# Two-layer decoder trunk: selection scores as stacked one-pass products, values two steps behind, first weight tiles in pieces

## What is computed

```python
s = jnp.einsum('bqghd,bgqkd->bghqk', qb, k_g) * scale      # selection
p = masked_softmax(s, valid)
o_sel = jnp.einsum('bghqk,bgqkd->bqghd', p.astype(v_g.dtype), v_g)
s = jnp.einsum('bqghd,bkgd->bghqk', qb, k_w) * scale       # window
s = jnp.einsum('bqghd,bngd->bghqn', qb, k_cmp) * scale     # compressed
o = gb[..., 0:1] * o_cmp + gb[..., 1:2] * o_sel + gb[..., 2:3] * o_win
```

## Time and profile before

| | |
|---|---|
| median of 3 runs | 720.13 us (717.53 to 721.34) |
| profiled execution | 720.99 us, its span 719.3 us |
| TensorE, share of the span busy | 96% |
| VectorE, ScalarE | 58%, 55% |
| granted TensorE clock, mean | 0.987 |
| sparse attention, four turns | 78.6 to 169.5 us |
| latent attention, four turns | 433.6 to 507.0 us |

### The profile page before, as it was taken

One profiled execution on the slowest core, in us unless ns is written; L12 is line 12 of the kernel. 1 busy time (PEld: TensorE's weight loads), 2 busy tenths in 40 slices (PEclk: granted clock), 3 DMA queues, 4 the chain that ended last, 5 costly groups with the idle time before them and its releaser, 6 DMA issues. The chain is left out here.

```text
span 719.3 us, 9969 instructions
## 1 busy us (share of the span) xinstructions
PE 687.6 (96%) x3553; PEld 576.6 (80%) x3553; DVE 415.7 (58%) x866; ACT 395.7 (55%) x779; POOL 13.2 (2%) x36
## 2 busy tenths in 40 slices
PE   5999899999999999999998999999999999999996
PEld 4888788778778888888887998877878888888885
DVE  4786545777665555455458675454575444445555
ACT  5785646677564344433366576685673334444443
POOL 5000000000000000000000000000000000000000
PEclk9999999999999999999999999997999999999999
DMA  8854305113355555555553353524227554445431
GB/s 299 285 155 124 92 4 176 59 60 118 102 191 176 175 178 185 201 196 195 201 161 120 100 158 125 176 67 133 96 91 243 191 175 176 175 175 175 175 117 58
DMA packets 54481, 108.92 MB, mean 151 GB/s; under 512 B 2273, under 2 KB 16657, under 8 KB 54449
## 3 DMA queue, kind: packets, MB, share of 16 engines
q1 hardware_dynamic: 53536, 105.73, 43.9%
q0 software_dynamic: 912, 2.78, 1.3%
HBM read 107.46 MB, written 1.05 MB: 151 GB/s over the span
## 5 line engine op out<-in xcount | busy, mean ns | idle before, releaser
L281 DVE TENSOR_TENSOR w_lo<-raw,w_hi 128x2048 fp32r<-128x2048 f32 (+6 forms) x111 | 207.8, 1887 | 71.7 <-ACT w_hi L273 71.5
L289 PE MATMUL bank<-w_hi,act_lo 128*128 128x512 f32 (+4 forms) x504 | 198.6, 394 | 5.4 <-DVE w_lo L1885 3.9
L291 PE MATMUL bank<-w_hi,act_hi 128*128 128x512 f32 (+4 forms) x504 | 189.4, 376 | 0.0
L290 PE MATMUL bank<-w_lo,act_hi 128*128 128x512 f32 (+4 forms) x504 | 189.3, 376 | 0.0
L273 ACT ACTIVATE w_hi<-raw 128x2048 fp32r<-128x2048 f32 (+6 forms) x111 | 174.1, 1589 | 10.0 <-PE bank L291 8.9
L289 PEld LDWEIGHTS bank<-w_hi,act_lo 128*128 128x128 f32 x504 | 95.9, 190 | 25.1 <-issue 7.7
L290 PEld LDWEIGHTS bank<-w_lo,act_hi 128*128 128x128 f32 x504 | 96.1, 191 | 17.5 <-issue 1.9
L291 PEld LDWEIGHTS bank<-w_hi,act_hi 128*128 128x128 f32 x504 | 95.7, 190 | 17.1
L1306 ACT ACTIVATE hidT_hi<-bank 128x512 fp32r<-128x512 f32 x20 | 12.0, 598 | 164.0 <-PE bank L768 164.0
L1728 DVE TENSOR_TENSOR hidT_lo<-bank,hidT_hi 128x512 fp32r<-128x512 f32 x20 | 13.8, 691 | 130.1 <-ACT hidT_hi L1306 130.1
L289 PE MATMUL bank<-w_hi,hidT_lo 128*128 128x512 f32 x160 | 63.3, 396 | 0.0
(11 more groups left out here) (214 smaller groups left out, 915.3 us busy)
## 6 DMA issues: line engine op xcount, KB each, us to landing
raw<-in_w_gate_up SPq DMA_DIRECT2D x44, 1024.0 KB, 5.2
raw<-in_w_down SPq DMA_DIRECT2D x22, 1024.0 KB, 4.9
raw<-in_nsa_w_in SPq DMA_DIRECT2D x5, 1024.0 KB, 6.3
raw<-in_w_q_up SPq DMA_DIRECT2D x8, 576.0 KB, 3.9
raw<-in_nsa_w_out SPq DMA_DIRECT2D x4, 1024.0 KB, 5.4
raw<-in_mla_w_out SPq DMA_DIRECT2D x4, 1024.0 KB, 5.2
raw<-in_mla_w_in SPq DMA_DIRECT2D x4, 768.0 KB, 4.5
raw<-in_nsa_w_in SPq DMA_DIRECT2D x6, 384.0 KB, 3.3
```

The lines of the kernel that those rows point to most:

```text
L281: ins = dve.tensor_tensor(lo[:, cols], raw[s][:, cols], hi[:, cols].bitcast(F32), ALU.subtract)
L289: pe.matmul(dst, a_lo, b_hi, start=start, stop=False)
L290: pe.matmul(dst, a_hi, b_lo, start=False, stop=False)
L291: return pe.matmul(dst, a_hi, b_hi, start=False, stop=stop)
```

## The change

Scores of the sparse layer: q is split into hi (fp32r) and lo, and both halves are stacked on 128 rows; the keys' hi is stored twice on 128 rows, their lo as well. One fp32r matmul over 128 rows gives (q_hi + q_lo) k_hi for both branches, one more per key tile adds the product with k_lo. The compressed keys are stacked alike and scored in one pass with both halves beside each other (30 columns), added by VectorE. The keys' halves are made on ScalarE and VectorE, transposed in two rounds of 16, and copied out by ScalarE in eight copies. ScalarE writes each turn's queries twice (four copies for two), VectorE makes the lo part (`q_low`). The query transposes move one step later, the last one into the next turn. Values are issued two steps behind the probabilities in both layers, with a third probability buffer. `out_factors` and `taken` move to step 6 in the sparse layer, the compressed exponential ahead of `exps`. At the start the first half of weight tile 0 is split in two pieces and tile 1 in two halves; TensorE issues 5 products of zeros ahead of the first transposes and 9 behind them, and GpSimd clears their operand first. GpSimd no longer clears `qT`, `kT` and `kcT`.

```diff
@@ start, GpSimd, TensorE, ScalarE, VectorE
+            pool.memset(zero[:].bitcast(F32), 0.0).then_inc(sem("zero"), 1)
-            for a in (qT[:], kT, kcT, cT, vbd):
+            for a in (cT, vbd):
+            pe.wait_ge(sem("zero"), 1)
+            idle_products(5)
+                if s == 0:
+                    idle_products(9)
+                            if s == 0 and t == 0:
+                                pe.wait_ge(sem("second_lo" if k else "first_lo"), 1)
+                        if s == 0 and t == 0 and k == 1:
+                            pe.wait_ge(sem("first_lo"), 2)
+            for k in range(2):
+                act.activation(w_hi[0][:, k * 512:(k + 1) * 512], raw[0][:, k * 512:(k + 1) * 512], ACT.Copy) \
+                    .then_inc(sem("first_hi"), 1)
-            split_hi(act, 1, SLOT)
+            split_hi(act, 1, SLOT, part=0).then_inc(sem("second_hi"), 1)
+            split_hi(act, 1, SLOT, part=1)
@@ def scores
+                    pe.matmul(dst, q, k_hi[:, turn, :, 0:keys], start=True, stop=False)
+                    for kt in range(t + 1):
+                        last = pe.matmul(dst[:, :, kt * P:(kt + 1) * P], q, (k_lo0, k_lo1)[kt][:, turn], start=False,
+                                         stop=kt == t)
@@ def cmp_scores
-                        last = pe.matmul(bank[5][:, at_:at_ + NCMP], queries["nsa"][turn % 2][:, i, t * P:(t + 1) * P],
-                                         kcT[:, turn * NCMP:(turn + 1) * NCMP], start=True, stop=True)
+                        last = pe.matmul(bank[5][:, at_:at_ + 2 * NCMP], queries["nsa"][turn % 2][:, i, t * P:(t + 1) * P],
+                                         kc_halves[:, turn].rearrange("p v n -> p (v n)"), start=True, stop=True)
@@ def attend, TensorE
+                    if turn * UNITS + n > 1:
+                        pe.wait_ge(sem(f"{m}_probsT"), turn * UNITS + n - 1)
-                    if unit > 0:
-                        values(m, unit - 1)
+                    if unit > 1:
+                        values(m, unit - 2)
@@ query transposes
+            def turn_nsa_queries(turn, n):
+                if n == 0 and turn > 0:
+                    turn_queries("nsa", turn, 3, turned_at(n))
+                if 1 <= n < 4 and turn < TURNS - 1:
+                    if n == 1:
+                        pe.wait_ge(sem("nsa_roped"), turn + 2)
+                    turn_queries("nsa", turn + 1, n - 1, turned_at(n))
@@ keys, TensorE and ScalarE
+            def turn_halves(half):
+                pe.wait_ge(sem("ks_halves"), half + 1)
+                for j in range(2 * T):
+                    b, t = divmod(j, T)
+                    for g in range(QUAD):
+                        last = pe.transpose(K_BANKS[4 * half + j][:, g * P:(g + 1) * P],
+                                            ks_halves[half][:, t, b * QUAD + g, :], ident[:])
+                    last.then_inc(sem("k_turned"), 1)
-            pe.wait_ge(sem("kT_out"), 1)
+            pe.wait_ge(sem("kT_out"), 4)
             turn_hidc(0)
+            turn_halves(1)
+            for t in range(T):
+                ins = copy(twice(ks_halves[0][:, t]).bitcast(F32R), to_both(kstage[:, t]))
@@ head of attention
+            block_values()
             pe.wait_ge(sem("nsa_roped"), 1)
...
-                    if turn == 0 and at_ == 0 and n == 0:
-                        block_values()
-                        pe.wait_ge(sem("nsa_q_out"), (turn + 2) * T)
+                        pe.wait_ge(sem("nsa_q_out"), (turn + 2) * 2 * T)
+            split_hi(act, NSA_Q1 + 3, 3 * KVW)
+            exps("nsa", 0)
+            exps("nsa", 1)
             q_out("nsa", 1, NSA_Q1 + 2)
@@ VectorE
+            def q_low(to):
+                hi, lo = (a.rearrange("p t i n -> p (t i) n") for a in q_halves(to))
+                dve.wait_ge(sem("nsa_q_out"), to * 2 * T + 2 * T)
+                chain.link(dve.tensor_copy(hi[:, :, 0:16].bitcast(F32R), lo[:, :, 0:16]))
+                dve.tensor_tensor(lo.bitcast(F32R), lo, hi, ALU.subtract).then_inc(sem("nsa_roped"), 1)
+            for t in range(T):
+                ins = dve.tensor_tensor(twice(ks_halves[1][:, t]).bitcast(F32R), to_both(kstage[:, t]),
+                                        twice(ks_halves[0][:, t]), ALU.subtract)
-                    if n == 7:
+                    if n == (6 if nsa else 7):
                         out_factors(m, turn, 0)
                         taken(m, turn, 0)
```

More of the change, by code:

```diff
@@ L56 @@
 SLOT = 2048
+BIG = 10208
 SEL_SCALE = HD ** -0.5
@@ L172, in trunk, with place @@
         newton = sb("newton", [P, 2])
-        with nc.sbuf_tensor("big", [P, 10240], F32) as big:
+        with nc.sbuf_tensor("big", [P, BIG], F32) as big:
             pass
+        with ExitStack() as within:
+            def place(name, shape, dt=F32):
+                return within.enter_context(nc.sbuf_tensor(name, shape, dt))
+            k_lo1 = place("k_lo1", [P, QUAD, 2, P], F32R)
+            k_hi = place("k_hi", [P, QUAD, 2, SEQ], F32R)
+            place("to_q_odd", [P, 3072])
+            q_odd = place("q_odd", [P, QUAD, SEQ], F32R)
         more_hi = [sb(f"more_hi{i}", [P, SLOT], F32R) for i in range(2)]
@@ L1002, in turn_keys, with idle_products @@
                 last.then_inc(sem("mla_k_turned"), 1)
+            def idle_products(count):
+                for _ in range(count):
+                    pe.matmul(bank[7][:], zero[:, 0:P], zero[:], start=True, stop=True)
             pe.wait_ge(sem("ident"), 1)
+            pe.wait_ge(sem("zero"), 1)
+            idle_products(5)
             def kv_block(b):
@@ L1538, in _ @@
                 .then_inc(sem("gelu_done"), 1)
+            for j in range(2 * T):
+                keys_halves_out(1, j)
             act.wait_ge(sem("hidc_turned"), 2)
@@ L1840, in attend @@
                         masked(m, turn * UNITS + n)
+                    if nsa and n == 0 and 0 < turn < TURNS - 1:
+                        q_low(turn + 1)
                     if turn > 0:
@@ L1883, in _ @@
             turn_dve(dve, 0, 0, [0])
-            dve.wait_ge(sem("first_hi"), 1)
-            dve.tensor_tensor(w_lo[0][:, 0:SLOT // 2], raw[0][:, 0:SLOT // 2], w_hi[0][:, 0:SLOT // 2].bitcast(F32),
-                              ALU.subtract).then_inc(sem("first_lo"), 1)
+            for k in range(2):
+                dve.wait_ge(sem("first_hi"), k + 1)
+                cols = slice(k * 512, (k + 1) * 512)
+                dve.tensor_tensor(w_lo[0][:, cols], raw[0][:, cols], w_hi[0][:, cols].bitcast(F32),
+                                  ALU.subtract).then_inc(sem("first_lo"), 1)
             turn_dve(dve, 0, 0, [1])
@@ L1889, in _ @@
             split_lo(dve, 0, SLOT, part=1)
-            split_lo(dve, 1, SLOT)
+            dve.wait_ge(sem("second_hi"), 1)
+            dve.tensor_tensor(w_lo[1][:, 0:SLOT // 2], raw[1][:, 0:SLOT // 2], w_hi[1][:, 0:SLOT // 2].bitcast(F32),
+                              ALU.subtract).then_inc(sem("second_lo"), 1)
+            dve.wait_ge(hi_ready, 2)
+            split_lo(dve, 1, SLOT, part=1)
             turn_dve(dve, 0, 1)
@@ L1980, in _ @@
             rotate("nsa", 0)
+            q_low(0)
             split_lo(dve, NSA_Q1 + 2, 2 * KVW)
```

235 lines of the change are left out of this document (129 added, 106 removed).

## The result

The changed kernel took 715.85 us (median of 7 runs, 710.98 to 716.94), the kernel before 720.83 us (7 runs): a ratio of 0.993, 95% interval 0.991 to 0.996. In a second series on another chip it was 714.12 us and 0.991 (0.989 to 0.993). So the change is faster by 5 to 6.5 us. 15.9 us were forecast, 704.2 us, with 712.0 as the range's upper end.

A forecast was written before the change was run, and what follows sets the result against it. TensorE, busy for 96% of the span, was taken as the bound. The terms summed to -15.9 us, from 720.99 to 705.1 us; that execution lay 0.9 us above its median, so 704.2 us, range 695.5 to 712.

The forecast's parts named there:

- Start, -1.5: Kernel's start: split weight tiles and zero products bring the first block's products earlier, 1.5 us less, 0 to 1.6.
- Keys in halves, +1.9: Ahead of sparse attention: a second round of 16 key transposes has no cover, 1.9 us more, from 1.7 to 3.4.
- head, -0.5: Head of sparse attention: transposes of step 1 start earlier, 0.5 us less, from 1.5 less to 1.5 more.
- Scores, -9.1: Sparse attention's score units: stacked fp32r matmuls instead of float32, 9.1 us less.
- compressed scores, -3.5: Sparse attention's compressed scores: one pass of eight records instead of sixteen, 0.88 us a turn, 3.5 us less in four.
- Waits, -4.7 + 3.4: Sparse turns: waits go, turn 1 keeps its clock, 4.7 us less; new waits 3.4 us, bounds 1 to 7.
- Latent attention, -1.9: Latent attention: values two steps behind remove four waits, 1.9 us less; at worst 0 us.
- A: Sparse attention: ScalarE and VectorE hold the turns, or the stacked matmul is slower, 711 us; chance 0.2.
- C: Sparse attention: without dense matmuls the clock falls, 729 us if 25 us of work run slow; chance 0.06.
- signs for A: Sparse attention in the profile after: turn 2 over 19.5 us, with waits for exponentials.
- B: Latent attention: its lost clock comes back, up to 6.9 us to be had, 697 us; chance 0.2.

The follow-up runs named there:

- e4: Changed kernel with VectorE's masks issued one unit earlier in both attention layers: 703.16 us, 0.977 of the kernel before.
- e12: Changed kernel with masks one unit earlier and the second output piece's lower half made at step 3 instead of 4: 701.60 us, repeated 700.10 us.
- e3: Changed kernel with each sparse score product made twice: 714.79 us, 0.994 of the kernel before.
- e5: Changed kernel with zero products in TensorE's waits in the head and first two turns of sparse attention: 711.41 us, 0.988 of the kernel before.
- e9: Kernel before the change with VectorE's masks issued one unit earlier in both attention layers: 711.31 us, 0.987 of the kernel before.

## Why the prediction was wrong, point by point

- **Start, -1.5.** Right in the trace: first product at 9.20, k = 2 at 12.22 (12.24 foreseen), k = 4 at 14.52 (14.65). In time it was worth 2.4 and 2.8 us where the masks didn't bind, with intervals that overlap, and nothing that can be seen on the change's own order.
- **Keys in halves, +1.9, and head, -0.5.** The product with the compressed keys, behind both rounds of key transposes, starts at 65.86 us after 65.88 before: -1.5 + 1.9 came out as 0.0, 0.4 better than summed, since the second round costs 1.7 us and the start gives 1.65. The first mask stands 0.76 us later (76.31 against 75.55) because `block_values` (0.9 us) now lies ahead of it. The fill of step 1 goes on at 81.52 (81.6 foreseen) behind 1.49 us of waiting, the transposes at 83.35 (83.3).
- **Scores, -9.1, compressed scores, -3.5.** Right: two products of a 256-column unit take 75.84 to 76.08, 0.24 us, the compressed scores 89.68 to 90.58, 0.9 us, and 13.4 us of work left the stretch (the sum said 12.6, and 0.9 us of `block_values` moved ahead of it, 13.5).
- **Waits, -4.7 + 3.4.** The step that failed. Of the 4.7, 3.0 were waits and 1.7 clock; so the sum had +0.4 for waits and -1.7 for the clock. Measured are +4.6 and +3.4, 9.3 us more, out of the 10.6 by which the profiled span missed (719.3 to 714.0, 5.3 us less). The mask waits were to go "since each gets either an earlier place on its engine or a step more of slack"; the first mask of a turn got rid of `taken` but not of the rope, the second stands behind the new `q_low` (1.10 us of waiting at 104.77), and the mask waits doubled, 1.5 to 3.1 us. The clock of turn 1 was to hold since the waits go; 10.2 us were slow where 3.6 had been. The working asked of each engine whether its work fits in the turn, found turn 2 tight, and added 1.5 us for it. It should have followed the mask of the next unit through VectorE's queue, past a rope that waits for ScalarE. With the old 3.0 gone the new waits are 7.6 us, 0.3 of them in the head, just over their upper bound of 7; the slow clock came on top. That the order of the queues is what sets these waits is shown by e4 and e12, which change nothing else; with it mended in both kernels 12.0 of the 15.9 us are there.
- **Latent attention, -1.9.** The four waits went, and mask waits came, as the bound "at worst 0" had it for exponentials: 75.2 us before, 74.9 in both of the change's profiles.
- **Rivals.** What happened is A (711 us), by queue order rather than by full engines, joined by a small part of C: slow clock took 5.1 us of the sparse attention, 3.4 more than before, where C had priced 25. The range ended at 712, since neither was let grow while both were true. Of the signs for A, turn 2 lasted 20.7 us (its line was 19.5), though its waits were for masks more than for exponentials. B's price was real, on another order: latent attention of e12, the same work with its masks and the output piece earlier, has no slow stretch and is 6.7 us shorter than before.

```profile
415.30:483.75 68.45, 63.12 (x401) 55.57 (x400) 37.52 (x145) 50.30 (x153) 0.00 (x0) 1.00 0.40 128
```

In the repeat of e12 6.8 us are slow there, and it lasts 71.3 us. The Trainium skill, page "TensorE: Matmul & The Clock Gate", part 4 "PE-mode transpose", says that transposes don't count as activity for the clock. The slow stretches went when score products (e3) or zero products (e5) were added to the same transposes, which fits that; but they also went with nothing added, when the masks came earlier (e9 and the repeat of e12), and no run tells transposes from the short values products.

Of the 3.9 us that are missing even with the queues in order, the two profiles show 2.7 as waits (3.1 more, where the sum had 0.4) and 1.9 as latent attention, which lasts 71.3 us in both; the start and the keys came out 0.5 better. Open: why values two behind bring more slow clock on the change's order, and how much of the clock's loss is due to waits and how much to fewer columns.

## What to carry to other kernels

Before pricing work that is taken off the bounding engine, follow the operation it waits for through the other engine's in-order queue: what stands ahead of it and what that waits for. An engine that is 71% busy in a stretch can hold one that is 89% busy there. A slope test (the same work done twice) tells in one run whether work counts: 2 us for 11.4 said no, but it sums up waits and clock, and the trace has to tell them apart. The cure was an order on VectorE worth twice the change. It was worth 9 us on the kernel before too, where the list of waits had shown 1.5 us for masks: try such an order before judging a change by its time.

## What was not expected of the hardware

TensorE's clock was a second price beside the idle time: in the change, 4.6 us more of waits came with 3.4 us more of slow clock, all of it behind clusters of waits (1.49; 1.17 and 0.73; 1.04; 1.59 and 1.27 us). And 11.4 us of added products brought the granted clock in the sparse attention from 0.94 to 1.00, which paid for 5.1 us of them. The pairing did not always hold. In latent attention waits rose from 5.0 to 7.3 us while the slow time fell from 13.8 to 10.2 us, and in e4's profile 6.8 us of waits in the sparse attention stand beside the same 10.2 us of slow time as 10.0 us do in the change's.
